# Between two transformer blocks: the norm's weight product made ahead of the root, and the scaling by the root shared by VectorE and ScalarE

## What is computed

```python
def rmsnorm(x, w):
    xf = x.astype(jnp.float32)
    y = xf * lax.rsqrt(jnp.mean(xf * xf, axis=-1, keepdims=True) + EPS)
    return (y * w.astype(jnp.float32)).astype(x.dtype)

x = x + y @ w_out                                    # first block
x = x + swiglu(rmsnorm(x, ffn_norm_w), w_gate, w_up, w_down)
h = rms_norm(x, mix_norm_g_2)                        # second block
...
x = x + merged @ w_out_2
h2 = rms_norm(x, ffn_norm_g_2)
```

## Time and profile before

| | |
|---|---|
| median of 3 runs | 692.93 us (692.89 to 693.02) |
| the profiled execution: time, span | 692.24 us, 690.5 us |
| its granted TensorE clock | 0.998 of full speed |
| TensorE matmuls and transposes | 683.4 us busy, 99% of the span |
| VectorE | 485.5 us, 70% |
| ScalarE | 413.3 us, 60% |
| GpSimd | 96.0 us, 14% |
| chain of work that ended last | TensorE 99% |

### The profile page before, as it was taken

One profiled execution on the slowest core, in us unless ns is written; L12 is line 12 of the kernel. 1 busy time (PEld: TensorE's weight loads), 2 busy tenths in 40 slices (PEclk: granted clock), 3 DMA queues, 4 the chain that ended last, 5 costly groups with the idle time before them and its releaser, 6 DMA issues.

```text
span 690.5 us, 9477 instructions
## 1 busy us (share of the span) xinstructions
PE 683.4 (99%) x3812; PEld 588.9 (85%) x3812; DVE 485.5 (70%) x739; ACT 413.3 (60%) x701; POOL 96.0 (14%) x163
## 2 busy tenths in 40 slices
PE   9999999999999999999999999999999999999996
PEld 8888888888888888888888988888888888888885
DVE  6878787768666666667465767777868877777774
ACT  7786765656555555546555866565567665555553
POOL 2124031688100000012710000000000000000001
PEclk9999999999999999999999999999999999999999
DMA  9946434746555555536434335554454655455401
GB/s 341 391 131 245 179 122 148 264 145 243 183 189 184 199 201 200 186 125 223 179 131 168 122 122 195 193 198 181 158 208 149 214 213 183 182 183 187 180 0 62
DMA packets 19484, 126.14 MB, mean 183 GB/s; under 512 B 2416, under 2 KB 2544, under 8 KB 5232
## 3 DMA queue, kind: packets, MB, share of 16 engines
q1 hardware_dynamic: 19296, 125.34, 50.3%
q10 hardware_dynamic: 144, 0.20, 0.1%
HBM read 124.48 MB, written 1.05 MB: 182 GB/s over the span
## 4 chain that ended last, share of the span: by engine, by line
PE 99%; DVE 0%; issue 0%; ACT 0%; POOLq 0%; POOL 0%
PE bank L222 95%; PE bank L231 3%; DVE xres L243 0%; POOLq L1526 0%; DVE last L243 0%; ACT last L234 0%; ACT junk L234 0%; POOL ss L248 0%; POOL ones L267 0%; POOL half L267 0%; POOLq L151 0%; POOLq L1594 0%
## 5 line engine op out<-in xcount | busy, mean ns | idle before, releaser
L243 DVE TENSOR_TENSOR wlo<-raw,whi 128x1024 fp32r<-128x1024 f32 x222 | 271.7, 1236 | 62.4 <-ACT whi L234 59.4
L234 ACT ACTIVATE whi<-raw 128x1024 fp32r<-128x1024 f32 x222 | 230.4, 1051 | 5.2 <-PE bank L222 3.8
L222 PE MATMUL bank<-xb,whi 128*128 128x512 f32 x496 | 124.2, 392 | 0.0
L222 PE MATMUL bank<-xa,whi 128*128 128x512 f32 x432 | 108.3, 393 | 0.0
L222 PEld LDWEIGHTS bank<-xb,whi 128*128 128x128 f32 x496 | 90.4, 188 | 17.4 <-DVE sg L243 0.2
L222 PE MATMUL bank<-whi,xb 128*128 128x512 f32 (+1 forms) x352 | 96.2, 355 | 0.0
L222 PEld LDWEIGHTS bank<-xa,whi 128*128 128x128 f32 x432 | 78.9, 188 | 15.7
L222 PEld LDWEIGHTS bank<-xb,wlo 128*128 128x128 f32 x496 | 67.6, 190 | 4.9
L222 PEld LDWEIGHTS bank<-whi,xb 128*128 128x128 f32 x352 | 62.1, 189 | 9.3 <-ACT vtok L234 0.3
L222 PE MATMUL bank<-xb,wlo 128*128 128x256 f32 x496 | 69.1, 282 | 0.0
L248 POOL TENSOR_SCALAR mean<-ss 128x1 f32<-128x1 f32 x7 | 2.3, 323 | 434.4 <-ACT xn L234 256.7
(11 more groups left out here) (244 smaller groups left out, 935.3 us busy)
## 6 DMA issues: line engine op xcount, KB each, us to landing
raw<-in_w_dram SPq DMA_DIRECT2D x109, 1024.0 KB, 4.8
first<-in_first_dram SPq DMA_DIRECT2D x8, 388.0 KB, 6.0
raw<-in_w_dram SPq DMA_DIRECT2D x4, 512.0 KB, 8.6
bias<-in_bias_dram SPq DMA_DIRECT2D x1, 1024.0 KB, 9.9
xres<-in_x_dram SPq DMA_DIRECT2D x1, 1024.0 KB, 8.2
gain<-in_ffn_norm_w_dram SPq DMA_DIRECT2D x1, 512.0 KB, 8.9
gain<-in_mix_norm_g_dram SPq DMA_DIRECT2D x1, 512.0 KB, 9.7
gain<-in_ffn_norm_g_dram SPq DMA_DIRECT2D x1, 512.0 KB, 5.1
```

What stands on the lines that cost most here:

```text
L222: return P(lambda e: e.matmul(o, l, r, start=start, stop=stop), *w, inc=inc)
L234: return A(lambda e: e.activation(o, i, f, **kw), *w)
L243: return q(lambda e: e.tensor_tensor(out=o, in0=a, in1=b, op=op), *w)
```

## The change

In `add_norm` the two scalar_tensor_tensor instructions on VectorE are replaced. Residual x gain is formed by two tensor_tensor instructions on VectorE, each waiting for the square of its half (which writes to the same place in `xn`). Once `rstd` is there, VectorE scales half 0 of `xn` in place (tensor_scalar) and ScalarE scales half 1 in place (activation with a scale). The function is called six times: three norms, two tiles.

```diff
-        norm_tok["x"] = [sqs[1]]
         g = ts(G, mean[:, t:t + 1], ss[:, 2 * t:2 * t + 1], ss[:, 2 * t + 1:2 * t + 2], EPS, ALU.add, ALU.add, sqs[1])
         g = inv_sqrt(rstd[:, t:t + 1], mean[:, t:t + 1], 1, g)
-        for hf in range(2):
-            c = slice(hf * 512, hf * 512 + 512)
-            norm_tok[t, hf] = stt(to[:, c], xres[:, t, c], rstd[:, t:t + 1], gains[slot][:, c], ALU.mult, ALU.mult,
-                                  g, gain_tok[name])
+        halves = [slice(0, 512), slice(512, 1024)]
+        weighted = [tt(V, to[:, c], xres[:, t, c], gains[slot][:, c], ALU.mult, sqs[hf], gain_tok[name])
+                    for hf, c in enumerate(halves)]
+        norm_tok["x"] = [sqs[1], weighted[1]]
+        r = rstd[:, t:t + 1]
+        norm_tok[t, 0] = ts(V, to[:, halves[0]], to[:, halves[0]], r, None, ALU.mult, None, g, weighted[0])
+        norm_tok[t, 1] = copy(to[:, halves[1]], to[:, halves[1]], g, weighted[1], scale=r)
```

## The result

| | before | changed |
|---|---|---|
| median (lowest to highest), 6 runs each | 692.90 us (692.14 to 693.02) | **695.21 us** (694.85 to 695.47) |
| ratio, with its 95% interval | | 1.0034 (1.0024 to 1.0045) |
| profiled execution: time, span | 692.24, 690.5 us | 695.05, 693.3 us |

What follows compares the result with a forecast made beforehand. TensorE was taken to bound the kernel, gaining only where it stands still. 3(r - 0.51) + 0.86 + 3r = 6r - 0.67, with r = 0.47 +2.15 us, gave a median of 695.1 us, range 693.0 to 696.0.

Steps and rivals of the forecast that it cites:

- The bound: TensorE, busy 99% of the span, bounds the kernel; a quicker `xn` can give about 1.05 us, at t = 1.
- The hold-up, r: Delay of the root's release, because VectorE's second product holds up `mean` on GpSimd: 0.47 us, bounds 0 and 0.63.
- The case in which `mean` does all its work only after the product: Rival: GpSimd begins `mean` only once VectorE's second product is done; delay 0.63, +3.11 us, 696.0; chance 0.09.
- My other overlap, near the start: Evidence for the block: root on GpSimd meets a VectorE split, takes 1.64 us instead of about 0.57, ends 0.59 after it.
- Term A: Transposes of t = 1: scaling after the root readies `xn` sooner; the matmul behind them shifts by r - 0.51 us per norm.
- Term B: ScalarE's queue at t = 0: scaling ahead of a weight split delays the norm of t = 1, in sum 0.86 + 3r.
- 6r - 0.67: Sum over the three norms of the transposes' gain and the queue's loss; with r = 0.47, +2.15 us.
- What hid: Transposes of t = 0 cost nothing: half 0 ready at 116.60, first transposes at 117.14; TensorE's `xa` wait, some 0.7 us, not added.
- The rival of an unhurt GpSimd: `mean` on GpSimd isn't held up, r near 0; only ScalarE's queue costs: -0.67, 692.3 us; chance 0.12.

Runs made afterwards that it cites:

- the two best kernels: Two kernels with half 0's product ahead of the root and `mean` on VectorE, half 0 scaled on ScalarE or on VectorE: 691.88 and 691.68 us.
- e1_order: Against the changed kernel: ScalarE's scaling of t = 0 moved behind the weight split; 692.98 us.
- e2_vector_both: Against the changed kernel: both halves scaled on VectorE, none on ScalarE; 692.90 us.
- e4_queue_only: Against the changed kernel: only half 0's product ahead of the root, scaled on ScalarE ahead of the weight split; half 1 by the old instruction; 693.21 us.
- e5_queue_order: Against the changed kernel: only half 0's product ahead, scaled on ScalarE, at t = 0 behind the weight split; half 1 by the old instruction; 692.38 us.
- the pair of probes: The kernel before plus one idle VectorE instruction behind the second square: with two SBUF inputs 695.43 us, with one input in PSUM 692.88 us.
- e11_half_and_mean: Against the kernel before: half 0's product ahead of the root, scaled on VectorE, half 1 by the old instruction, `mean` on VectorE; 691.68 us.
- e6_probe_sbuf: The kernel before plus one idle VectorE product with both inputs in SBUF, behind the second square; 695.43 us.

## Why the prediction was right

- *The bound.* TensorE's busy time did not move (683.6 against 683.4), and the whole gain that I said was to be had, 1.05 us, is what the two best kernels brought.
- *The hold-up, r.* Put at 0.47, measured at 0.49 at t = 0 (and 1.58 against 1.08 at t = 1, 0.50). `mean` ended 0.18 and 0.16 after the product; I had taken 0.16 from the last norm. The case in which `mean` does all its work only after the product (r = 0.63, the Trainium skill's "fully blocks" to the letter; of two SBUF inputs it says this in that page's summary table) didn't come, though GpSimd started just 0.06 after VectorE. My other overlap, near the start, was set against the wrong row: 0.57 is the root's time for 128 x 1, and by it the 0.59 behind the split would be all of the work. That root is 128 x 2, and a power of that form, not held up, takes 0.72 in the trace of before, so some 0.13 had been done by then, much as in the last norm. The row:

```profile
L243 POOL TENSOR_TENSOR vst<-vst,half 128x2 f32<-128x2 f32 x1 | 0.7, 715 | 0.1
```

- *Term A, r - 0.51 per norm.* By itself in `e1_order` and `e2_vector_both` it came to -0.03 in sum, where -0.12 was predicted. The gain was as worked out: in the changed kernel the matmul behind the eight transposes starts 1.39 after the root (124.23 to 125.62), before it was 1.89 (122.59 to 124.48). But r at t = 1 was 0.50 and not 0.47, three times over.
- *Term B, 0.86 + 3r.* The first subtraction started 2.85 after the root in the first norm (116.55 to 119.40), as worked out, and 2.85 again in the other two. Without r it measured 0.83, from `e4_queue_only` against `e5_queue_order`.
- *The sum.* 6r - 0.67 with the measured 0.49 is 2.27; the stretches show 2.33, the medians 2.31.
- *What hid.* The transposes of t = 0 were not late in the changed kernel, but there was less to spare than I took from the 117.14 of the earlier trace rows: their loads come up 0.23 ahead of them, and in the second norm the first load was 0.08 late, without holding up its transpose. The loads waited for `xa` by 0.76, 0.90 and 0.73 in the three norms, where I had said 0.7.
- *What I did not foresee* is in the frame and not in the sum: the profiled execution of before was early. The chain in order of time of the changed kernel starts with a load:

```profile
0.79 3.58 DMA first<-in_first_dram
...
25.67 0.87 PE bank L231 x8
```

The first transposes of before stood at 25.27, so 0.4 us of the 2.8 between the two spans lies ahead of everything that was changed. The forecast for the median does not suffer from this, since I moved it from the profiled execution's 692.24 to the median's 692.93.

The rival of an unhurt GpSimd would have given 692.3. It is refuted by `mean` itself, at 0.79 us, and by the pair of probes, and not only by the time, which a loss of another origin could have given as well.

## What to carry to other kernels

Work moved ahead of a wait isn't free because its engine was idle: look at what the engine that produces the awaited value reads just then. On this chip a VectorE instruction with two inputs in SBUF, begun beside a tiny GpSimd instruction, lengthened that from 0.32 to 0.81 us, and one with an input in PSUM did not. And before handing a scaling to a second engine, read which instruction stands behind it in that engine's stream and who waits for that one: here the place in the queue, ahead of or behind one weight split, decided between a loss of 2.3 us and none.

## What the runs showed of the hardware that I had not expected

- How long VectorE had been at work when GpSimd began hardly matters to what is left of `mean` afterwards: with VectorE 0.06 to 0.07 us ahead `mean` ended 0.16 to 0.19 after VectorE's instruction, and with VectorE about 0.4 ahead, in the last norm, 0.16 too. In the probes the VectorE instruction itself took 0.69 both times, whether GpSimd was held up or not.
- The start of the program varies: the first loads for the transposes of the first norm lie at 116.75 us in the profile of before and at 117.5 to 117.8 in those of eight of the experiments (117.17 in `e11_half_and_mean`; in the ninth other one, `e6_probe_sbuf`, they wait for the norm), though TensorE has the same stream up to there and waits for no norm. That is as much as one of the finer steps here is worth, which is why those were read from stretches of the trace.
